# Down projections of a hybrid encoder step in 2x2 blocks: seven products in place of eight

## The reference

```python
D_MODEL, D_FF, CONV_W = 1024, 2816, 3

def conv_ffn(h, past, w_up, conv_w, conv_b, w_down):
    T = h.shape[1]
    a = h @ w_up                                  # (T, 2 * D_FF)
    full = jnp.concatenate([past, a], axis=1)
    c = conv_b
    for j in range(CONV_W):
        c = c + conv_w[j] * full[:, j:j + T]
    g = c[..., :D_FF]
    up = c[..., D_FF:]
    return (jax.nn.silu(g) * up) @ w_down, full[:, T:]
```

## Time and profile before

| | us |
|---|---|
| median of 3 runs | 1678.91 |
| lowest, highest | 1678.46, 1679.55 |
| the profiled execution, its own time | 1676.94 |
| its span, first to last instruction | 1675.0 |
| PE busy | 1617.9 (97%) |
| DVE busy | 927.9 (55%) |
| ACT busy | 621.4 (37%) |
| POOL busy | 168.1 (10%) |

### The profile page before, as it was taken

The page is one execution under the profiler, slowest core; times in us unless marked ns, Lnnn a source line. Parts: engine busy times, 40 slices in busy tenths (PEclk is TensorE's granted clock), DMA queues, the critical chain, the costliest instruction groups (busy, mean ns, idle before and its releaser), DMA issues.

```text
span 1675.0 us, 25851 instructions
## 1 busy us (share of the span) xinstructions
PE 1617.9 (97%) x11138; PEld 1548.9 (92%) x11138; DVE 927.9 (55%) x1287; ACT 621.4 (37%) x928; POOL 168.1 (10%) x270
## 2 busy tenths in 40 slices
PE   7999878999999999999999999999999999999998
PEld 7759835799999999999999999999999999999998
DVE  5278877445665266526656715537663566346653
ACT  4546434734332133213354433324331233123441
POOL 2000000012110011001121100021110011001200
PEclk9999989999999999999999999999999999999999
DMA  5212445011222222221231221321222122211321
GB/s 217 80 50 77 153 179 201 26 58 69 76 76 76 76 76 72 80 76 56 75 112 70 92 83 55 113 76 64 72 72 95 52 76 76 101 51 63 114 92 48
DMA packets 27938, 143.52 MB, mean 86 GB/s; under 512 B 3392, under 2 KB 7104, under 8 KB 14640
## 3 DMA queue, kind: packets, MB, share of 16 engines
q1 hardware_dynamic: 26912, 139.03, 23.5%
q0 software_dynamic: 768, 2.81, 0.5%
q10 hardware_dynamic: 144, 0.02, 0.0%
HBM read 136.29 MB, written 5.43 MB: 85 GB/s over the span
## 4 chain that ended last, share of the span: by engine, by line
PE 92%; DVE 3%; ACT 2%; issue 1%; DMA 0%; SPq 0%; ACTq 0%; DVEq 0%
PE psum L634 71%; PE psum L680 9%; PE psum L720 2%; PE psum L551 1%; PE psum L490 1%; PE psum L583 1%; PE psum L499 1%; PE psum L590 1%; PE psum L538 1%; PE psum L669 1%; PE psum L510 1%; PE psum L565 1%; ACT a_hi L973 1%; DMA xT<-in_xT 0%; PE psum L759 0%
## 5 line engine op out<-in xcount | busy, mean ns | idle before, releaser
L634 PE MATMUL psum<-a_hi,w_hi 128*128 128x384 f32 (+2 forms) x1920 | 439.2, 310 | 7.5 <-DVE a_lo L1283 7.5
L634 PE MATMUL psum<-a_hi,w_lo 128*128 128x384 f32 (+2 forms) x1920 | 437.8, 309 | 0.0
L634 PE MATMUL psum<-a_lo,w_hi 128*128 128x384 f32 (+2 forms) x1920 | 437.7, 309 | 0.0
L634 PEld LDWEIGHTS psum<-a_hi,w_hi 128*128 128x128 f32 x1920 | 341.8, 188 | 9.6 <-issue 6.7
L634 PEld LDWEIGHTS psum<-a_hi,w_lo 128*128 128x128 f32 x1920 | 342.3, 188 | 0.0
L634 PEld LDWEIGHTS psum<-a_lo,w_hi 128*128 128x128 f32 x1920 | 342.2, 188 | 0.0
L1277 DVE TENSOR_TENSOR w_lo<-w_raw,w_hi 128x2048 fp32r<-128x2048 f32 (+1 forms) x101 | 227.3, 2250 | 120.7 <-ACT w_hi L970 120.6
L970 ACT ACTIVATE w_hi<-w_raw 128x2048 fp32r<-128x2048 f32 (+1 forms) x102 | 189.6, 1858 | 171.8 <-PE psum L634 171.8
L634 PE MATMUL psum<-g_hi,w_hi 128*128 128x320 f32 x832 | 191.2, 311 | 2.4 <-DVE u_act L1489 1.6
L1126 ACT ACTIVATE conv<-conv_in,convw 128x656 f32<-128x656 f32 x88 | 82.4, 937 | 293.4 <-DVE conv_in L1523 293.4
L634 PE MATMUL psum<-g_hi,w_lo 128*128 128x320 f32 x832 | 190.1, 310 | 0.0
(11 more groups left out here) (227 smaller groups left out, 1948.5 us busy)
## 6 DMA issues: line engine op xcount, KB each, us to landing
w_raw<-in_weights SPq DMA_DIRECT2D x93, 1024.0 KB, 4.8
key_b<-in_keyT SPq DMA_DIRECT2D x8, 1024.0 KB, 7.6
val_b<-in_val SPq DMA_DIRECT2D x8, 1024.0 KB, 4.8
w_raw<-in_weights SPq DMA_DIRECT2D x8, 768.0 KB, 4.2
kidx_b<-in_kidxT SPq DMA_DIRECT2D x8, 512.0 KB, 3.6
xT<-in_xT SPq DMA_DIRECT2D x2, 1280.0 KB, 7.1
out_yT<-xT SPq DMA_DIRECT2D x8, 320.0 KB, 2.2
xT<-in_xT SPq DMA_DIRECT2D x3, 640.0 KB, 8.3
```

The costliest lines, as they stand in the source:

```text
L634: last = pe.matmul(psum[:, 2 * j + bank, 0:t1 - t0], w[:, k, P * j:P * j + P], x[:, k, t0:t1], start=(k == 0 and n == 0), stop=(k == K - 1 ...
```

## The change

The down projections take 2x2 blocks: pairs of output chunks by pairs of hidden chunks by the two halves of the tokens (320 each). A block needs seven products of 128 x 128 by 320 in place of eight. For that the seven left operands are three blocks of the weights and four sums of blocks (`weight_sum`: s = 3, 4, 2, 6), and the seven right operands three blocks of `hidden` and four sums (`hide_even`, `hide_odd`). Each is split into hi and lo by itself. Products 0, 2, 4 and 6 go on adding up in one PSUM bank, and DVE takes the bank's state out to x after each (`add_seven`); the next of them waits for that.

- A down unit with K chunks is 7 x K/2 x 3 matmuls. `PARTS` becomes `(4, 6, 6, 6)`, so that every part is even.
- The order of units: the first up unit of the next part comes ahead of the four down units of each part but the last (`ffn_order`).
- The seven weight blocks of a unit lie in a ring of ten blocks over both slots; a block is split once the product ten places back is done.
- The unit after a down phase is split in two halves (`split_lo_half`).
- In the sample attention the values from b = 3 on are loaded from ACT's queue (`take_out`), no longer from SP's.
- Buffers are moved in SBUF, and the root of the mean square is written where its inverse goes.

```diff
-PARTS = (8, 8, 6)
+PARTS = (4, 6, 6, 6)
...
+def ffn_order():
+    last = len(PARTS) - 1
+    out = [("up", 0, i) for i in range(PARTS[0])]
+    for q in range(len(PARTS)):
+        if q < last:
+            out.append(("up", q + 1, 0))
+        out += [("down", q, i) for i in range(4)]
+        if q < last:
+            out += [("up", q + 1, i) for i in range(1, PARTS[q + 1])]
...
+        def block_free(eng, u, s):
+            u0, n, _ = group_of(u)
+            g = SEVEN * n + s
+            if g >= RING:
+                eng.wait_ge(product, n_product[u0 + (g - RING) // SEVEN, (g - RING) % SEVEN])
+            else:
+                before = u0 - 2 if g < HALF_RING else u0 - 1
+                eng.wait_ge(product, n_product[before, products_of[before] - 1])
...
-                if b >= KV:
-                    sp.wait_ge(out_ready, n_out_ready[S0 + b - KV])
-                sp.dma_start(val_b[b % KV][:, 0:8, :], val_in[b]).then_inc(s_val[b % KV], 16)
-                sp.dma_start(val_b[b % KV][0:TQ, 8, :], vtok[TQ * b:TQ * b + TQ, TT - 1, :]).then_inc(s_val[b % KV], 16)
+                if b < KV:
+                    sp.dma_start(val_b[b][:, 0:8, :], val_in[b]).then_inc(s_val[b], 16)
+                    sp.dma_start(val_b[b][0:TQ, 8, :], vtok[TQ * b:TQ * b + TQ, TT - 1, :]).then_inc(s_val[b], 16)
             sp.wait_ge(logits, n_logits[S1 - 1])
...
-                ahead = ready and UNITS[u][0][:4] == "down"
-                if ahead:
-                    for j in range(2):
-                        free(u, j)
-                        part(j, range(K - 1))
...
+            def product_seven(u, l, q):
+                u0, n, _ = group_of(u)
+                half = UNITS[u][2] // 2
+                sum_bank, one_bank, two_bank = (6, 4, 5) if n % 2 == 0 else (2, 0, 1)
+                c0 = off_part[q]
+                for s in range(SEVEN):
+                    pe.wait_ge(w_lo_ready, n_w_lo_ready[u, s])
+                    if s == 0 and n == 1:
+                        free(u0, 1)
+                    if s == 0 and n >= 2:
+                        pe.wait_ge(free_dve, n_free_dve[u - 2, 6])
+                    if s in (2, 4, 6):
+                        pe.wait_ge(free_dve, n_free_dve[u, s - 2])
+                    if s == 5:
+                        pe.wait_ge(free_dve, n_free_dve[u, 3])
+                    bank = {1: one_bank, 3: two_bank, 5: two_bank}.get(s, sum_bank)
+                    wh, wl = (chunked_block(w) for w in ring_block(u, s)[0:2])
+                    for m in range(half):
+                        if n == 0:
+                            pe.wait_ge(h_lo, n_h_lo[l, c0 + 2 * m + (s > 0)])
+                        for i, (w, x) in enumerate(((wh, b_hi), (wh, b_lo), (wl, b_hi))):
+                            last = pe.matmul(psum[:, bank, 0:HT], w[:, m, :], x[:, s, m, :],
+                                             start=(s in (0, 1, 3) and m == 0 and i == 0),
+                                             stop=(m == half - 1 and i == 2), skip_group_check=True)
+                    last.then_inc(product, 1)
...
+                    b = a + KV
+                    act.dma_start(val_b[b % KV][:, 0:8, :], val_in[b]).then_inc(s_val[b % KV], 16)
+                    act.dma_start(val_b[b % KV][0:TQ, 8, :], vtok[TQ * b:TQ * b + TQ, TT - 1, :]).then_inc(s_val[b % KV], 16)
...
+                def hide_even(c, m):
+                    act.wait_ge(h_ready, n_h_ready[l, c])
+                    act.activation(b_hi[:, 0, m, :], hidden[0][:, 0:HT], ACT.Copy).then_inc(h_hi, 1)
+                def hide_odd(c, m):
+                    act.wait_ge(h_ready, n_h_ready[l, c])
+                    act.activation(b_hi[:, 1:7:5, m, :], halves(hidden[1][:, :]), ACT.Copy).then_inc(h_hi, 1)
+                    act.wait_ge(h_sum, n_h_sum[l, c])
+                    act.activation(b_hi[:, 2:6, m, :], b_sum[:, 2:6, m, :], ACT.Copy).then_inc(h_hi, 1)
...
                             if i == 2:
                                 act.wait_ge(s_p, 16 * (l + 1))
                                 act.activation(p_hi[:, :, :], p_raw[:, :, :], ACT.Copy).then_inc(p_hi_ready, 1)
+                            act.wait_ge(free_dve, n_free_dve[u, 6])
                             for n in (2 * i, 2 * i + 1):
-                                act.wait_ge(free_dve, n_free_dve[FIRST[f"down{l}{q}"] + i, n % 2])
...
+            def split_seven_lo(u, s):
+                hi, lo, total = (chunked_block(w) for w in ring_block(u, s))
+                dve.wait_ge(w_hi_ready, n_w_hi_ready[u, s])
...
+                def hide_even(c, m):
+                    dve.wait_ge(h_ready, n_h_ready[l, c])
+                    dve.tensor_tensor(b_sum[:, 4, m, :], hidden[0][:, HT:T], hidden[0][:, 0:HT], ALU.subtract)\
+                       .then_inc(h_sum, 1)
+                    dve.wait_ge(h_hi, n_h_hi[l, c, 0])
+                    dve.tensor_tensor(b_lo[:, 0, m, :], hidden[0][:, 0:HT], f32(b_hi[:, 0, m, :]), ALU.subtract)\
+                       .then_inc(h_lo, 1)
...
+                def hide_odd(c, m):
+                    dve.wait_ge(h_sum, n_h_sum[l, c - 1])
+                    dve.wait_ge(h_ready, n_h_ready[l, c])
+                    link(dve.tensor_tensor(b_sum[:, 2, m, :], hidden[1][:, HT:T], b_sum[:, 4, m, :], ALU.subtract))
+                    dve.tensor_tensor(b_sum[:, 3, m, :], hidden[1][:, HT:T], hidden[0][:, HT:T], ALU.subtract)
+                    dve.tensor_tensor(b_sum[:, 5, m, :], hidden[1][:, 0:HT], b_sum[:, 2, m, :], ALU.subtract)\
+                       .then_inc(h_sum, 1)
+                    dve.wait_ge(h_hi, n_h_hi[l, c, 0])
+                    dve.tensor_tensor(b_lo[:, 1:7:5, m, :], halves(hidden[1][:, :]), f32(b_hi[:, 1:7:5, m, :]), ALU.subtract)
+                    dve.wait_ge(h_hi, n_h_hi[l, c, 1])
+                    dve.tensor_tensor(b_lo[:, 2:6, m, :], b_sum[:, 2:6, m, :], f32(b_hi[:, 2:6, m, :]), ALU.subtract)\
+                       .then_inc(h_lo, 1)
...
+                def add_seven(u, s, i):
+                    sum_bank, one_bank, two_bank = (6, 4, 5) if i % 2 == 0 else (2, 0, 1)
+                    bank, n, h = ((sum_bank, 0, 0), (one_bank, 0, 0), (sum_bank, 1, 0), (two_bank, 1, 1), (sum_bank, 1, 1),
+                                  (two_bank, 1, 0), (sum_bank, 0, 1))[s]
+                    dve.wait_ge(product, n_product[u, s])
+                    if s:
+                        dve.wait_ge(free_dve, n_free_dve[u, s - 1])
+                    x = xT[:, 2 * i + n, HT * h:HT * h + HT]
+                    dve.tensor_tensor(x, psum[:, bank, 0:HT], x, ALU.add).then_inc(free_dve, 1)
...
+                for kind, q, i in ffn_order():
+                    u = unit_of[f"{kind}{l}{q}", i]
+                    nxt = u + 1
...
+                        if nxt in by_seven:
+                            for s in (3, 4, 2):
+                                weight_sum(nxt, s)
+                            for s in (0, 1):
+                                split_seven_lo(nxt, s)
+                        else:
+                            split_lo(nxt)
...
+                        if nxt in by_seven:
+                            weight_sum(nxt, 6)
+                            for s in (2, 3, 4):
+                                split_seven_lo(nxt, s)
...
+                            if nxt in by_seven:
+                                split_seven_lo(nxt, 5 + j)
...
+                        if i % 2:
+                            hide_odd(c, i // 2)
+                        elif not (q and i == 0):
+                            hide_even(c, i // 2)
+                    else:
...
+                        seven = nxt in by_seven
+                        if seven:
+                            split_seven_lo(nxt, 0)
+                            split_seven_lo(nxt, 1)
+                        add_seven(u, 0, i)
+                        if seven:
+                            weight_sum(nxt, 3)
+                        add_seven(u, 1, i)
+                        if seven:
+                            weight_sum(nxt, 4)
+                            weight_sum(nxt, 2)
+                        add_seven(u, 2, i)
+                        add_seven(u, 3, i)
+                        if seven:
+                            weight_sum(nxt, 6)
+                            for s in (2, 3):
+                                split_seven_lo(nxt, s)
+                        else:
+                            split_lo_half(nxt, 0)
+                        add_seven(u, 4, i)
+                        if seven:
+                            for s in (4, 5):
+                                split_seven_lo(nxt, s)
+                        else:
+                            split_lo_half(nxt, 1)
+                        add_seven(u, 5, i)
+                        if seven:
+                            split_seven_lo(nxt, 6)
+                        add_seven(u, 6, i)
```

225 lines of the change are left out of this document (156 added, 69 removed).

## The result

| | before, us | after, us |
|---|---|---|
| median of the runs beside each other | 1679.23 | 1763.1 |
| lowest, highest (4 runs each) | 1678.46, 1681.96 | 1761.04, 1764.35 |
| the profiled execution, its own time | 1676.94 | 1762.61 |
| its span | 1675.0 | 1760.9 |
| mean granted clock | 0.988 | 0.959 |

The change made the kernel slower: ratio 1.0495, 95% interval 1.0478 to 1.0512. The forecast of 1754 was 9 us too low; the time lies inside the range. For the profiled executions, which the sum was made for, +75 was forecast and +85.7 measured.

A forecast was written before the change was run, and what follows sets the result against it. PE was taken to bound the kernel, busy 97% of the span. Terms -38.8 + 43 + 23 + 26 + 6 + 20 - 4 = +75 on 1676.94 gave 1752, and 1754 for the median; range 1732 to 1784.

The forecast's parts named there:

- Matmuls, -38.8: Down projections of both layers: 264 matmuls fewer at 0.147 us each, -38.8 us.
- First down unit behind the up unit ahead: Three per layer: PE waits 7.3 us, or 7.0 for K = 4, for DVE's addition before product 2; +43 us.
- First down unit of the last part: One per layer, no up unit ahead: PE stands 10.6 us within product 1, then 1.0 more; +23 us.
- Between its down units: Three places per layer in the last part: PE waits 4.4 us each for the addition before product 2; +26 us.
- Steady units: Down units without the long waits: K = 6 costs 0, at most +8 us; K = 4 costs +6 us.
- Up units: Odd up units get 2.9 us more DVE work, with 0.4 us of cover left: 0, +6 us otherwise.
- The clock, 13 x 1.6 = 20: PE's clock drops behind 13 of the 14 new waits, 1.6 us each: +20 us, bounds 0 and 23.
- The values, -4: Attention: with values off SP's queue, keys no longer wait behind them; -4 us, bounds 0 and -5.
- The rival that the seven products save nothing: Down projections: each product is bound by its weight load, so nothing is saved; 1793 us, chance 0.02.
- DVE as the bound everywhere: Rival: DVE becomes the bound in every down phase; about 1781 us, chance 0.15.
- Shorter stretches with the clock held: Rival: PE's new waits are shorter and few drop the clock; 1734 us, chance 0.12.
- the faster case: Rival: PE does not wait at part ends, kernel at 1636 us; faster below a 3 us mean over 14 stretches; chance 0.03.

The follow-up runs named there:

- experiment 2: Changed kernel with product 6's matmuls issued once more in each down unit, result unused, no further additions: 1795.98 us.
- experiment 4: Changed kernel with DVE's order changed at part ends: convolution chain moved into or behind the last down unit's additions, additions ahead of lower parts not yet needed: 1714.19 us.
- experiment 1: Changed kernel with extra, unused PE matmuls filling most of its waits to keep the clock up: 1739.4 us.
- Experiments 6 and 9: 6: kernel before with only the values moved to ACT's queue, 1674.24 us. 9: changed kernel with values back on SP's queue, 1769.99 us.
- The repaired kernels: Changed kernel with DVE reordered at part ends and eight products in the last part: 1653.19 us with parts 6, 6, 6, 4; 1656.94 with 4, 6, 6, 6.

## Why the prediction was right, and where it was off

*Matmuls, -38.8.* Right: the weight loads are 264 fewer, the up units still run at 576 in 84.6 to 84.8 us, and experiment 2, which adds nothing but the matmuls, gave 32.9 of the 38.8 back. The rival that the seven products save nothing is out.

*First down unit behind the up unit ahead, 7.3 and 7.0.* Measured 7.04, 7.03 and 6.85 in layer 0 and the same in layer 1: 42 us for the forecast 43. The cause is the forecast one, DVE's queue ahead of the first addition, as experiment 4 shows: let that addition stand ahead of the convolution chain and the lower parts, and six waits go.

*First down unit of the last part, 10.6 + 1.0.* Measured 10.4 and, behind it, 0.2: 21 in place of 23. *Between its down units, 4.4 each.* Measured 3.88, 4.55 and 4.01 in layer 0: 25 in both layers for 26. The rule of the Trainium skill (SBUF — State Buffer, section "SBUF: two separate sides") would have made these three 5.4 each. The rows of after at the place of the 4.55, from the timeline:

```profile
880.54 3.64 POOL L1871 TENSOR_TENSOR square_sum<-square_sum,square 128x640 f32<-128x640 f32 x2 [12.88 <-ACT square L1097]
...
881.22 3.65 DVE L1460 SCALAR_TENSOR_TENSOR a_lo<-xT,gains,a_hi 128x640 fp32r<-128x640 f32 x2 [1.53 <-ACT a_hi L1090]
```

Two a_lo rows took 3.65 us (1.57 and 2.15 one by one), where two that run alone take 1.76, and each ended 0.7 after the POOL row that it met. That agrees with the rule: the second began at 882.72 and POOL's row of 1.93 us ended at 884.18, so it stood beside most of that row. The first met a POOL row that was nearly half done, and the place cost 4.55 and not 5.4.

*Steady units.* K = 6: 0 forecast, and no wait in the table. K = 4: 6 forecast, measured 0.47 + 0.25 + 0.25 + 0.41 and 0.41 ahead of the up unit, 1.8 a layer, 3.6. *Up units*: 0 forecast, none found.

*The clock, 13 x 1.6 = 20.* This term was mis-sized. All 14 waits dropped it, the 3.88 us one too, and each cost 1.8 and not 1.6: 25.5 in the windows, of which experiment 1 gave 23 back. I had taken the length of the spell from one place; here it ranged from 2.9 us (479.30 on) to 5.4 (886.40 on). The Trainium skill (TensorE: Matmul & The Clock Gate, section "Why this matters for your kernels") warned of just this: by it all 14 would fall, and they did; that section gives no price per drop, and at the 1.6 of my row it came to 22.

*The values, -4.* Experiments 6 and 9 measured -5.3 and -5.9 to -6.9, beyond my bound of -5 by the medians and inside it by the profiled executions (3.6 and 4.4). In after, though, little of it reached the first up unit: the output projection starts 3.5 us earlier (337.06 for 340.55), but the clock, which there stayed up in the kernel before, fell. Windows of after:

```profile
334.00:337.00 3.00, 0.33 (x1) 0.14 (x1) 0.91 (x2) 2.55 (x6) 0.00 (x0) 0.74 0.00 0
337.00:340.00 3.00, 2.94 (x11) 2.97 (x12) 3.00 (x5) 3.00 (x6) 0.00 (x0) 0.50 0.00 0
```

*Terms that the sum lacked.* In the timeline the first matmul of the unit at 618.44 starts 0.34 after the last of the unit before, in place of 0.147, and the next one 0.22 after it: the 9.47 for 9.26 above. Gaps of 0.30 to 0.36 stand at 22 places in the down units of both layers, each at the start of a unit or of one of its products: with the 0.22 behind them 0.26 each, some 6 us. I had given them nothing, since the blocks of the earlier trace rows run through. Which instruction makes them (the waits at a unit's start are more than before) I did not try. And each of the 14 large waits costs 0.3 us more than the view says, 4 us in all: it counts from the end of the last matmul, whose row is 0.31 long where the next start would come after 0.147, and the second matmul behind the wait comes 0.13 late (0.40 for 0.267 at 602.05).

The balance of the profiled spans, which differ by 85.9: matmuls -38.8, waits of PE in both feed-forward parts +92 (46 a layer, without the 0.8 ahead of the first up product), clock +25.5, the gaps +6, the ends of the waits +4, and -1.1 for an earlier start of the feed-forward (400.71 for 401.84). The first five make 89; from the first up product of a layer to its last projection it is 43.7 more in layer 0 and 45.6 in layer 1, 89.3. Between the two (867.8 to 1131.53 before, 910.4 to 1171.84 after) it is 2.3 less. Of that 1.6 is the spell at 0.50 of the earlier trace rows: in after the same wait of 1.63 us stands at 1059.75, and the clock stayed at 1.00 (1059.8 to 1062.8).

So the forecast came within 11 us of the profiled execution in part by luck. The waits came out 6 lower than the sum had them and that stretch 2 lower; the clock was 5 higher, the gaps and the ends of the waits 10, and of the values' 4 only 1 arrived.

*The rivals.* DVE as the bound everywhere (0.15) is out by experiment 4: with the same DVE work the six waits vanish. Its time, 1781, was 18 us too high as well. Shorter stretches with the clock held (0.12) is out by the windows. For the faster case (0.03) the point was a mean wait under 3 us; it was 6.3 (88 us in 14). The repaired kernels do what that rival said, 17 and 21 us above its 1636, of which 7.1 and 10.6 are products given back; the small waits that PE still has in their feed-forward parts come to 9.2 and 8.0, and the rest is open.

## What to carry to other kernels

A scheme that trades matmuls for vector rows can fit by its totals and still lose, since what decides is which vector rows stand in the queue ahead of the one that frees the next product. Count that queue at each place where the kind of work changes, and move what nobody waits for yet (here the convolution of a channel block that is first read one unit of products later) behind what TensorE asks for next, and let the row that frees a product stand ahead of rows that prepare later ones. Where no other work can stand ahead, as in a layer's last part, keep the old form: there the saved matmuls (10.6 us) cost 65.
